# The first MLP's down product: 16 of its 32 inner tiles by seven block products, modulation rows in groups of four

## The reference

```python
h = h + jnp.square(jax.nn.relu(hn @ w_up[layer])) @ w_down[layer]     # first block, inner width 4096
...
mod = jax.nn.silu(c) @ w_ada + b_ada                                  # third block: 6 x 1024 numbers
...
f = jnp.square(jax.nn.relu(h @ w_fc1)) @ w_fc2                        # third block, inner width 4096
```

## Time and profile before

| what | value |
|---|---|
| median of 3 runs | 3313.03 us (3308.84 to 3313.93) |
| profiled execution, its own time | 3316.2 us |
| its span, first to last instruction | 3314.2 us |
| mean granted clock of TensorE | 0.993 |

### The profile page before, as it was taken

How to read it: one execution, slowest core, us unless ns; L and a number is a source line. 1 busy time by engine, 2 the same in 40 slices (tenths; PEclk the granted TensorE clock), 3 DMA queues, 4 the chain that set the end, 5 groups by cost and what they waited for, 6 DMA issues and landing times.

```text
span 3314.2 us, 40211 instructions
## 1 busy us (share of the span) xinstructions
PE 3255.0 (98%) x16118; PEld 2648.4 (80%) x16118; DVE 2008.5 (61%) x2966; ACT 1299.0 (39%) x2014; POOL 1288.5 (39%) x768
## 2 busy tenths in 40 slices
PE   8999999999999999998999999999999999999998
PEld 6788888888888878875687888888888888887887
DVE  4563347665564538577558888776536485655553
ACT  5332233333121221176535545521223364456652
POOL 3112324555353213231424554554212215555963
PEclk9999999999999999999999999999999999999999
DMA  3011312235554212111022222366111132247743
GB/s 111 31 58 65 127 51 96 110 117 191 177 206 165 96 39 70 57 66 42 5 98 70 77 82 90 107 230 231 58 59 45 39 133 108 110 158 241 238 149 121
DMA packets 142502, 358.36 MB, mean 108 GB/s; under 512 B 15958, under 2 KB 58726, under 8 KB 142188
## 3 DMA queue, kind: packets, MB, share of 16 engines
q1 hardware_dynamic: 142316, 355.79, 30.8%
HBM read 292.66 MB, written 63.09 MB: 107 GB/s over the span
## 4 chain that ended last, share of the span: by engine, by line
PE 90%; DVE 5%; ACT 2%; DMA 1%; POOL 1%; issue 0%; SPq 0%; POOLq 0%; DVEq 0%; ACTq 0%
PE ps L751 16%; PE ps L752 16%; PE ps L754 16%; PE ps L809 9%; PE ps L811 9%; PE ps L810 9%; PE ps L842 2%; PE ps L843 2%; PE ps L844 2%; PE ps L993 1%; PE ps L1216 1%; PE ps L784 1%; PE ps L786 1%; PE ps L785 1%; PE ps L1265 1%; PE ps L1249 1%
## 5 line engine op out<-in xcount | busy, mean ns | idle before, releaser
L3512 POOL TENSOR_TENSOR wlo<-raw,whi 128x1024 fp32r<-128x1024 f32 (+3 forms) x162 | 388.6, 2399 | 1174.8 <-ACT whi L1499 1174.8
L751 PE MATMUL ps<-HH,whi 128*128 128x512 f32 (+2 forms) x1520 | 607.1, 399 | 2.3 <-DVE HL L2358 1.4
L752 PE MATMUL ps<-HL,whi 128*128 128x512 f32 (+2 forms) x1520 | 597.1, 393 | 0.0
L1499 ACT ACTIVATE whi<-raw 128x1024 fp32r<-128x1024 f32 (+3 forms) x164 | 163.2, 996 | 817.3 <-PE ps L754 789.6
L754 PE MATMUL ps<-HH,wlo 128*128 128x512 f32 (+2 forms) x1536 | 476.6, 392 | 0.0
L3582 POOL TENSOR_TENSOR wlo<-raw,whi 128x512 fp32r<-128x512 f32 x188 | 275.0, 1464 | 281.4 <-ACT whi L1596 240.2
L754 PEld LDWEIGHTS ps<-HH,wlo 128*128 128x128 f32 (+2 forms) x1536 | 287.3, 187 | 66.0 <-issue 1.1
L751 PEld LDWEIGHTS ps<-HH,whi 128*128 128x128 f32 (+2 forms) x1520 | 285.0, 188 | 67.0 <-issue 3.0
L752 PEld LDWEIGHTS ps<-HL,whi 128*128 128x128 f32 (+2 forms) x1520 | 284.9, 187 | 61.9 <-issue 2.0
L2342 DVE TENSOR_TENSOR T<-T,ps 128x512 f32<-128x512 f32 (+1 forms) x254 | 174.3, 699 | 231.1 <-PE ps L811 192.4
L2342 DVE TENSOR_TENSOR X<-ps,X 128x1024 f32<-128x1024 f32 (+1 forms) x91 | 108.1, 1188 | 313.9 <-PE ps L754 296.8
(11 more groups left out here) (514 smaller groups left out, 6624.8 us busy)
## 6 DMA issues: line engine op xcount, KB each, us to landing
raw<-in_w_up SPq DMA_DIRECT2D x76, 512.0 KB, 4.1
WF<-in_w_fc SPq DMA_DIRECT2D x72, 512.0 KB, 4.5
raw<-in_w_in SPq DMA_DIRECT2D x62, 512.0 KB, 3.3
hsc<-T SPq DMA_DIRECT2D x62, 512.0 KB, 2.7
GF<-hsc SPq DMA_DIRECT2D x42, 512.0 KB, 5.8
raw<-in_w_down SPq DMA_DIRECT2D x40, 512.0 KB, 5.3
raw<-in_w_fc SPq DMA_DIRECT2D x40, 512.0 KB, 4.0
T<-in_w_ada SPq DMA_DIRECT2D x32, 512.0 KB, 3.8
```

Of the source, the lines that this page charges most:

```text
L751: e.matmul(o_[0:m, half(hf)], whi_[k], hi[k0 + k][:, half(hf)], start=first, stop=False)
L752: e.matmul(o_[0:m, half(hf)], whi_[k], lo[k0 + k][:, half(hf)], start=False, stop=False)
L1499: e.activation(whi_of(name), v3(raw_of(name), 2) if name in SPLIT else raw_of(name), ACT.Copy).then_inc(*ac.inc("hi " + name))
L3512: e.tensor_tensor(wlo_of(name), raw_of(name), whi_of(name).bitcast(F), SUB).then_inc(*po.inc("lo " + name))
```

## The change

The first MLP's groups 0 to 2 (16 inner tiles, jobs 0 to 23) become a stream of seven products of 8 steps, right behind `fast_all("up")`. Jobs 24 to 39 stay; job 24 takes its tiles in the order 4 to 7, 0 to 3. All functions of the stream get the MLP's name `t` as an argument. The 48 rows go in 12 groups of four after jobs 24 to 32, 34, 36 and 38 (`ROWQ`), and a group's weights come as four parts (`row_load`). In both streams the first loads are issued in another order, and on DVE the sum of weights goes behind the low part; step 3's sum goes from DVE to POOL in the third MLP. Weight places now hold their two blocks apart (`wplace`).

```diff
-ADAS = [[0]] + [[2 * n - 1, 2 * n] for n in range(1, 9)] + [[n + 8] for n in range(9, 24)] + [[2 * n - 16, 2 * n - 15] for n in range(24, 32)] + [[]] * 8
-assert sum(ADAS, []) == list(range(48))
+ROWQ = {24 + n: n for n in range(9)} | {34: 9, 36: 10, 38: 11}
...
-NK = 12
...
-WPLACE = [0, 1, 2, 0] + [(3, 1, 2, 0)[v % 4] for v in range(4, 36)] + [3, 1, 2, 3, 1, 2]
-
-
-def sum_on_vector(s):
-
-    return s // NK == 2 or s in (3, 5, 7, 9, 11)
-
+NK = {"up": 8, "fa1_": 12}
+G0 = {"up": 3, "fa1_": 4, "fup": 0}
+NSTEP = {t: len(BLOCKS) * NK[t] for t in NK}
...
+WPLACE = {"up": [0, 4, 2, 0] + [(1, 3, 2, 0)[v % 4] for v in range(4, 27)] + [1],
+          "fa1_": [0, 1, 2, 0] + [(3, 1, 2, 0)[v % 4] for v in range(4, 36)] + [3, 1, 2, 3, 1, 2]}
...
+
+
+def sum_on_vector(t, s):
+
+    b = s // NK[t]
+    return (b == 2 and (t == "fa1_" or s % 2 == 1)) or (b == 0 and s > 4 and s % 2 == 1)
...
-SPLIT = ("dn0_0", "fdn0_0")
+SPLIT = ("fdn0_0",)
...
-        AR = [T[1], RT, T[2]]
+        AR = [RT, T[0], T[1], T[2]]
...
+        wplace = {"fa1_": [(WO, WO + 4096), (TO + 4096, TO + 8192), (WO + 8192, WO + 12288), (RO, TO)],
+                  "up": [(WO + 4096, WO + 8192), (TO + 4096, TO + 8192), (WO + 12288, WO), (RO, TO), (GO + 49152, GO + 53248)]}
...
+                    ks=[4, 5, 6, 7, 0, 1, 2, 3] if (t, n) == ("up", 24) else None)
...
-                for f in rows.pop(0):
-                    if f == 0:
-                        q.wait_ge(*ac("n2 rt"))
-                    q.wait_ge(*dv(f"red ada{f}"))
-                    row(f)
-                rows.append(ADAS[n] if n >= 0 else [])
+                for g in rows.pop(0):
+                    for f in range(4 * g, 4 * g + 4):
+                        q.wait_ge(*dv(f"red ada{f}"))
+                        row(f)
+                rows.append([ROWQ[n]] if n in ROWQ else [])
...
-            for n in range(40):
+            blocks("up")
+            for n in range(24, 40):
...
+                if t == "up":
+                    if s in (46, 48, 50, 52):
+                        k = 4 + (s - 46) // 2
+                        high(f"dnh {16 + k}", HF[:, k, :], HH[:, k, :], dma[f"hr{8 + k}"](f"uphr {16 + k}"))
+                    elif s == 53:
+                        highs(widx["dn3_0"])
+                    return
...
+            for k in range(4):
+                high(f"dnh {16 + k}", GXF[:, k, :], HH[:, k, :], dma[f"hr{8 + k}"](f"uphr {16 + k}"), pe(f"upS {52 + k}"))
+            for n in range(24, 40):
...
-                if sum_on_vector(s + 1):
-                    q.wait_ge(*wload_of(s + 1))
-                    tt(wblock(s + 1, 0), wblock(s + 1, 0), wblock(s + 1, 1), ADD, f"S sW {s + 1}")
-                if s < NSTEP:
-                    block_sum(s)
...
+
+            def block_step(t, s):
+
+                if s < NSTEP[t]:
+                    block_sum(t, s)
                 if s:
-                    block_low(s - 1)
-                if s > NK and s % NK in (3, 4):
-                    block_out(s // NK - 1, s % NK - 3)
-                if s > 69 and s % 4 == 2:
+                    block_low(t, s - 1)
+                if s + 1 < NSTEP[t] and sum_on_vector(t, s + 1):
+                    q.wait_ge(*wload_of(t, s + 1))
+                    tt(wblock(t, s + 1, 0), wblock(t, s + 1, 0), wblock(t, s + 1, 1), ADD, f"{t}S sW {s + 1}")
+                if s > NK[t] and s % NK[t] in (3, 4):
+                    block_out(t, s // NK[t] - 1, s % NK[t] - 3)
+                if t == "up":
+                    if s in (50, 54):
+                        k = 5 + (s - 50) // 2
+                        q.wait_ge(*ac(f"dnh {16 + k}"))
+                        tt(HL[:, k, :], HF[:, k, :], HH[:, k, :].bitcast(F), SUB, f"dnl {16 + k}")
...
+                if n not in ROWQ:
+                    return
+                g = ROWQ[n]
+                part_ = v3(misc[:, 512:1024], 4)
                 for k in range(8):
...
+                    u = row_tile_of(g, k // 2)
+                    w_ = AR[u][:].rearrange("p (f k m) -> p k f m", f=4, k=2)[:, k % 2]
+                    if k % 2 == 0:
+                        q.wait_ge(*dma[f"ar{u}"](f"ada {g} {k // 2}"))
+                    done_ = [f"adar {g} {k // 2}"] if k % 2 else []
+                    if k == 0:
+                        if g:
+                            q.wait_ge(*dv(f"red ada{4 * g - 1}"))
+                        e.tensor_scalar(part_, w_, SC[:, 0:1], None, MUL).then_inc(*dv.inc(f"row{g} 0"))
+                        continue
+                    q.wait_ge(*dv(f"row{g} {k - 1}"))
+                    if k < 7:
+                        stt(part_, w_, SC[:, k:k + 1], part_, MUL, ADD, f"row{g} {k}", *done_)
+                        continue
+                    if g:
+                        q.wait_ge(*pe(f"row{4 * g - 1}"))
+                    stt(adat[:], w_[:, 0:2], SC[:, 7:8], part_[:, 0:2], MUL, ADD, f"red ada{4 * g}", f"red ada{4 * g + 1}")
+                    stt(adat2[:], w_[:, 2:4], SC[:, 7:8], part_[:, 2:4], MUL, ADD, f"red ada{4 * g + 2}", f"red ada{4 * g + 3}", *done_)
...
-            for n in range(40):
+            for k in (1, 3):
+                q.wait_ge(*ac(f"dnh {16 + k}"))
+                tt(HL[:, k, :], GXF[:, k, :], HH[:, k, :].bitcast(F), SUB, f"dnl {16 + k}")
+            block_out("up", 6, 0)
+            block_out("up", 6, 1)
+            for n in range(24, 40):
                 g, j = divmod(n, 8)
-                if g:
-                    q.wait_ge(*dv(f"dn x{g - 1} {j}"))
+                q.wait_ge(*dv(f"dn x{g - 1} {j}"))
                 to_x(f"dn{g}_{j}", j, f"dn x{g} {j}")
...
+                if t == "up":
+                    if s in (48, 52):
+                        k = 4 + (s - 48) // 2
+                        low(f"dnl {16 + k}", HF[:, k, :], HH[:, k, :], HL[:, k, :], ac(f"dnh {16 + k}"))
+                    elif s == 55:
+                        lows(widx["dn3_0"])
...
+            def weight_load(t, v):
+
+                p = WPLACE[t][v]
+                prior = [u for u in range(v) if WPLACE[t][u] == p]
+                if prior:
+                    q.wait_ge(*pe(f"{t}S {2 * prior[-1] + 1}"))
+                elif p == 0:
+                    q.wait_ge(*pe(f"{t}28"))
+                    q.wait_ge(*pe(f"{t}29"))
+                elif p == 1:
+                    q.wait_ge(*spilled(t, 28 if t == "fa1_" else 30))
+                    q.wait_ge(*spilled(t, 29))
+                elif p == 2:
+                    q.wait_ge(*pe(f"{t}30"))
+                    q.wait_ge(*pe(f"{t}31"))
+                elif p == 3:
+                    q.wait_ge(*spilled(t, 31))
+                    q.wait_ge(*dv(f"{t}c12 15"))
                 else:
...
+                    q.wait_ge(*pe(f"{t}15 p6"))
...
+            def blocks1():
+
+                for v in range(3, NSTEP["up"] // 2):
+                    if v == 27:
+                        loads(widx["dn3_1"])
+                    if v > 3:
+                        weight_load("up", v)
+                    for k in (2 * (v - 5) % 8, 2 * (v - 5) % 8 + 1):
+                        if 4 < v < 9:
+                            block_load("up", 1, 0, k, pe("up15 p4"))
+                        elif 8 < v < 13:
+                            block_load("up", 1, 1, k, pe("up15 p7"))
+                        elif 20 < v < 25:
+                            block_load("up", 0, 1, k, pe("upS 3"))
+                    if 12 < v < 17:
+                        k = v - 9
+                        q.wait_ge(*pe("up15 p3"))
+                        q.wait_ge(*spilled("up", 16 + k))
+                        load(f"hr{8 + k}", HF[:, k, :], hsc[16 + k], f"uphr {16 + k}")
+                    elif v > 23:
+                        k = v - 24
+                        q.wait_ge(*dv(f"upS sT {4 * NK['up'] - 1}"))
+                        q.wait_ge(*spilled("up", 16 + k))
+                        load(f"hr{8 + k}", GXF[:, k, :], hsc[16 + k], f"uphr {16 + k}")
...
+                    if v in (3, 4):
+                        for k in (2 * v + 2, 2 * v + 3):
+                            block_load("fa1_", 0, 0, k, pe("fa1_15 p6"))
...
-                    if (t, n) == ("fa1_", z):
-                        for k in range(4):
-                            block_load(0, 0, k, pe("fa1_15 p5"))
-                        weight_load(1)
-                        for k in range(4, NK):
-                            block_load(0, 0, k, pe("fa1_15 p5" if k < 8 else "fa1_15 p6"))
-                        weight_load(2)
-                        weight_load(3)
+                    if t in NK and n == z - 1:
+                        weight_load(t, 0)
+                    if t in NK and n == z:
+                        for k in range(8):
+                            block_load(t, 0, 0, k, pe(f"{t}15 p5"))
+                            if k in (1, 3, 5):
+                                weight_load(t, (k + 1) // 2)
...
+            def row_load(g, *ks):
+
+                for k in ks:
```

(61 more changed lines are left out.)

325 lines of the change are left out of this document (144 added, 181 removed).

## The result

The changed kernel took **3319.0 us** (median of 20 executions, 3310.6 to 3330.7), the one before 3310.6 in the same rounds (20, 3305.8 to 3320.9): ratio **1.0025, interval 1.0016 to 1.0033**, slower by 5 to 11 us. The forecast was 3292.8, range 3287 to 3305. It was wrong, and on the wrong side.

What follows compares the result with a forecast made beforehand. TensorE (PE), busy for 98% of the span, was taken as the bound; -21.8 - 1.0 - 0.3 + 2.5 + 0.5 - 0.3 = -20.4 us from a median of 3313.03 gave 3292.8 us, range 3287 to 3305.

Steps and rivals of the forecast that it cites:

- Fewer matmuls: First MLP: 768 matmuls become 672; 96 fewer at 0.2267 us each save 21.8 us.
- Rows four at a time: The 48 modulation rows in the last 16 jobs: twelve groups of four at 0.94 us save 1.2, counted as 1.
- D: Rival: the clock falls after the one-column matmuls of the row groups; twelve falls give 3334 us; chance 0.04.
- C: Rival: rows are supplied too slowly, PE paced by SP's loads in jobs 24 to 32; 3325 at 200 GB/s; chance 0.05.
- Jobs 33 to 39: Last jobs, where DVE also makes the next layer's operand beside the row groups: +0.5 us, bounds 0 and 4.
- Start of the new stream: First steps of the first MLP's new stream: waits for late loads and a possible clock fall, +2.5 us, bounds 0 and 6.6.
- The 1.7 at step 5: New stream's start: PE waits 1.7 us for POOL's low part of step 5, behind a late pair's weight sum.
- The 0.5 for the second wait: New stream near step 8: 0.5 us for weights and half tiles that come behind the spills of tiles 30 and 31.
- Inside the stream: New stream after its start: POOL's work and the load rate, 276 GB/s against 337 seen, cost 0.
- Third MLP's begin: Start of the third MLP's stream, first loads and DVE work reordered: -0.3 us, bounds -2 and +1.5.
- B: Rival: the starts and the last rows give back 9.4 us more, 3302 us; chance 0.17.
- E: Rival: POOL bounds the new stream if every weight sum takes 1.80 us, 7.9 us over products 4 to 6; chance 0.07.

Runs made afterwards that it cites:

- the early version: Changed kernel with SP asking two to four pairs of weights earlier for the first MLP stream's half tiles of products 2, 3 and 6: 3295.7 us, ratio 0.9953.
- the counter-test: The kernel before, with only `v - 3` made `v - 7` in the third MLP's half-tile loads: ratio 1.0026 to before, third stream 244.8 us.
- the version with both edits: Changed kernel with half tiles asked for earlier in the first MLP's stream and at the old places in the third's: 3293.9 us, ratio 0.9942.
- first MLP only: Changed kernel with only the first MLP stream's half tiles of products 2, 3 and 6 asked for earlier: 3295.7 us, ratio 0.9953 to before.
- third MLP's begin as before: Two kernels with both streams' half tiles early, the whole third MLP or only SP's order at its begin put back: 3291.5 and 3291.4 us.
- The kernel with the third MLP as before: Kernel with the first MLP's half tiles asked for early and the whole third MLP as in the kernel before: 3291.5 us, ratio 0.9939.
- The version with the spill first: Both streams' half tiles early, plus the spill of hidden tile 31 ahead of the third pair of weights on SP in both: 3294.1 us, ratio 0.9955.

## Why the prediction was wrong

*Fewer matmuls, -21.8:* right, 96 fewer. (The last step of the sum, 3295.8 - 3.2, is 3292.6, not 3292.8.)

*Rows four at a time, -1.0, and D and C:* right to the hundredth. The mechanism is as told: DVE stands before the first `adat` operation, PE nowhere, the clock stays at 1.00. From group to group (1005.14 to 1016.96) it is 11.82 us, a job of 10.88 and **0.94** for the group, 11.3 for twelve, as forecast.

```profile
1005.14 0.95 PE L1076 MATMUL ps<-ones,adat 128*128 128x1 f32 x8
1005.95 0.48 PE L764 MATMUL ps<-HH,whi 128*128 128x512 f32 x1
...
1016.96 0.95 PE L1076 MATMUL ps<-ones,adat 128*128 128x1 f32 x8
...
1006.20 0.87 DVE L2360 SCALAR_TENSOR_TENSOR adat<-T,SC,ps 128x256 f32<-128x256 f32 x2 [4.21 <-PE ps L1076]
...
1120.46 0.87 DVE L2360 SCALAR_TENSOR_TENSOR adat<-T,SC,ps 128x256 f32<-128x256 f32 x2
1121.37 1.28 DVE L2373 SCALAR_TENSOR_TENSOR HL<-X,gprod,HH 128x1024 fp32r<-128x1024 f32 x1
```

*Jobs 33 to 39, +0.5, bound 4:* nothing (PE busy 181 of 181). The seven operand tiles took 1.28 or 1.29 us each, never 3.42, as 1121.37 shows; none of them began while POOL worked. The rule of the Trainium skill that made the bound (SBUF — State Buffer, "Who interferes with whom") had almost no case here. Two POOL operations began in the last 0.4 us of an operand tile (at 1104.16 and 1127.10) and took 2.6 us where the others took 2.4, which does not contradict it.

*Start of the new stream, +2.5, bounds 0 to 6.6:* as the kernel stands 5.4 us at steps 5 and 7, inside the bounds, and the clock's fall behind them takes about 1.6 more, 7.0 in all, just outside. The 1.7 at step 5 came (1.85, at the place and from the engine foretold, though ACT's late half tile held it: POOL's sum had ended at 801.90, and its low part waited until 803.41 for ACT). The 0.5 for the second wait was mis-sized by two things that were in the code: the sum of step 8 stands ahead of the low part of step 7 on DVE, and PE wants step 7 half a step early, by `BORDER`. With early half tiles the whole stream costs 2.1 beyond its matmuls.

*Inside the stream, 0.* **This is the step that failed.** It weighed the work of POOL and the rate of the transfers, 276 GB/s against 337, and over a stage both had room, as the early version shows. (The loads are 1.57 MB per pair of steps, 289 GB/s, not 276.) It didn't ask when each half tile is asked for and what stands behind it. Some 10 us were lost here: the 16.0 of all waits less 5.4 at steps 5 and 7 and 0.5 at step 1. With the loads early they are 0.

*Third MLP's begin, -0.3, bounds -2 and +1.5:* the other half of the same failure. The sentence costed the order of the first loads, read from the order on SP, and passed over the shift from `v - 3` to `v - 7` a few rows on. It cost +8.8 and +8.0 in two traces, far out of the bounds; the counter-test gives the shift alone, +9.6 (7.9 of it waits). The reordering proper was mis-signed: about +2.

*The rivals:* B named the starts, E POOL as bound, C the rows; none was this one. E's condition did not occur: none of POOL's 34 sums of weights in the changed kernel's first stream (780 to 970) took more than 1.32 us, and with early half tiles POOL is busy for 75.72 of the 88.6 us from 855 to 943.6 while PE never stands.

The sum closes, if the clock is counted too. The first MLP's part of the table ends in the norm, where 32 one-column matmuls are followed by a fall of the clock in all 13 traces. It costs 3.4 us in some of them (the before, and the version with both edits) and 1.7 in others. Windows over the norm, before and with the first MLP's half tiles early:

```profile
1167.00:1184.00 17.00, 17.00 (x83) 14.74 (x82) 1.07 (x6) 1.67 (x4) 2.34 (x1) 0.80 0.01 2
...
1140.00:1154.50 14.50, 14.27 (x75) 12.30 (x76) 1.25 (x8) 1.63 (x3) 3.26 (x2) 0.88 0.02 3
```

With the half tiles early the part takes 365.4 (first MLP only), 367.1 (both), 365.2 and 364.5 (third MLP's begin as before) against 387.9. With the fall taken out of each that is **-20.9, -20.8, -21.0 and -21.8**, where my terms gave -20.1, or -21.0 with 2.1 measured for the start and 0 for the jobs. The kernel with the third MLP as before is at 0.9939 of the before, 20 us under it. The mechanism of the change was priced well; the loads that feed it were not priced at all.

*The time of the changed kernel.* The stages of the traces make it 3 to 4 us slower (-5.6 + 8.8, -3.8 + 8.0), the 20 executions 5 to 11. The difference between the two is granted clock. Span times mean granted clock, an estimate of what an execution would take without its falls, is 3293.0 us on the mean of the 20, and 3288.6 to 3289.8 for the before in the three rounds of the experiments (16, 11 and 14 executions): 3 to 4 us, as the stages say. The mean granted clock itself was 0.9925 against 0.9934 to 0.9941, and 0.001 of the span is 3.3 us. (For the before beside the 20 it was not recorded.)

One part of this can be seen. Each of the three traces with late half tiles in the first MLP has a fall inside the new stream, right behind a wait of 3.35, 2.61 and 3.46 us, and it costs 1.7 us each time:

```profile
813.00:818.00 5.00, 5.00 (x17) 3.93 (x16) 3.39 (x6) 4.21 (x9) 2.57 (x2) 0.66 0.14 52
841.00:846.00 5.00, 4.39 (x12) 3.49 (x13) 2.48 (x4) 2.84 (x6) 3.27 (x4) 0.66 0.58 203
815.00:820.00 5.00, 5.00 (x15) 3.94 (x16) 3.17 (x5) 4.20 (x8) 2.57 (x2) 0.66 0.31 116
```

The version with the spill first has one too, behind its 3.72 us; the seven other versions have none there. Not every such wait is followed by one (3.27 us at 816 of the second trace is not). Where the other falls of the changed kernel come from stays open.

The Trainium skill (TensorE: Matmul & The Clock Gate, Part 1) says that a lack of activity takes the full clock away; these rows agree, and no run here isolates it.
